# Gate of the DeltaNet group: tangent and products made per tile in the projection stage, squares and sums of its output norm per pair of tiles

## What is computed

```python
def deltanet_group(qkv, z, ab, ..., conv_w, a_log, dt_bias, norm_g, with_ctx_out):
    y = jax.nn.silu(short_conv(qkv_, conv_w))            # 5 taps over the tokens, 768 channels
    q, k, v = split(y);  q, k = l2norm(q) * 64 ** -0.5, l2norm(k)
    ...
    o_f, o_b = gated_delta_chunked(forward), gated_delta_chunked(flipped)
    def out(o, z_):                                      # o: 4 heads of 64
        o = rms_norm(o.transpose(0, 2, 1, 3), norm_g) * jax.nn.silu(z_).reshape(b_, t_, DN_HEADS, DN_HEAD_DIM)
        return o.reshape(b_, t_, DN_W)
    y = out(o_f + _flip_t(o_b), z)
```

## Time and profile before

| | us |
|---|---|
| median of 3 runs | 4419.28 (4417.69 to 4423.97) |
| the profiled execution | 4419.74 |
| span of its trace | 4417.9 |
| TensorE busy | 3963.3 (90%) |
| VectorE busy | 2058.3 (47%) |
| ScalarE busy | 1144.2 (26%) |
| GpSimd busy | 963.7 (22%) |
| mean granted TensorE clock | 0.942 of full |

### The profile page before, as it was taken

How to read it: one execution, slowest core, us unless ns; L and a number is a source line. 1 busy time by engine, 2 the same in 40 slices (tenths; PEclk the granted TensorE clock), 3 DMA queues, 4 the chain that set the end, 5 groups by cost and what they waited for, 6 DMA issues and landing times. The chain is left out here.

```text
span 4417.9 us, 77329 instructions
## 1 busy us (share of the span) xinstructions
PE 3963.3 (90%) x33040; PEld 3259.8 (74%) x33040; DVE 2058.3 (47%) x3681; ACT 1144.2 (26%) x2465; POOL 963.7 (22%) x671
## 2 busy tenths in 40 slices
PE   6999989789977999999996999889799788999997
PEld 4556877678865888888884657778688666888885
DVE  3344555444456433333356344566344554443346
ACT  3344223223322111111114443232233412111012
POOL 0000100033203333333321000100223114444441
PEclk8898999889988999999997999999799898999999
DMA  4211000100010111111111210000100010111111
GB/s 168 111 77 58 20 30 11 65 2 3 3 48 10 39 39 38 38 38 38 38 37 48 77 77 30 20 20 20 46 3 3 21 38 29 48 47 47 47 48 57
DMA packets 26495, 180.98 MB, mean 41 GB/s; under 512 B 2528, under 2 KB 4832, under 8 KB 10976
## 3 DMA queue, kind: packets, MB, share of 16 engines
q1 hardware_dynamic: 24912, 173.69, 10.6%
q10 hardware_dynamic: 1296, 3.10, 0.2%
HBM read 168.39 MB, written 8.39 MB: 40 GB/s over the span
## 5 line engine op out<-in xcount | busy, mean ns | idle before, releaser
L1291 PE MATMUL ps<-Yn_parts,ring_parts 128*128 128x512 f32 (+1 forms) x3840 | 802.1, 370 | 11.0 <-issue 7.7
L1291 PE MATMUL ps<-temp_parts,ring_parts 128*128 128x512 f32 (+1 forms) x2560 | 731.3, 371 | 55.8 <-DVE Hn_parts L2423 54.3
L1291 PEld LDWEIGHTS ps<-Yn_parts,ring_parts 128*128 128x128 f32 x3840 | 671.6, 190 | 138.3 <-issue 9.5
L1291 PEld LDWEIGHTS ps<-temp_parts,ring_parts 128*128 128x128 f32 x2560 | 468.1, 190 | 140.5 <-DVE Hn_parts L2423 55.7
L2694 POOL TENSOR_TENSOR ring_parts<-ring,consts 128x2048 fp32r<-128x2048 f32 x64 | 295.8, 4622 | 1200.9 <-DMA ring<-in_ff 1200.9
L735 PE MATMUL ps<-ring_parts,Xn_parts 128*128 128x256 f32 x2560 | 510.9, 295 | 51.4 <-DVE Hn_parts L1996 17.7
L2373 DVE SCALAR_TENSOR_TENSOR Xn<-ps,mods,Xn 128x256 f32<-128x256 f32 (+1 forms) x360 | 250.9, 697 | 623.1 <-PE ps L1291 514.3
L1291 PE MATMUL ps<-Hn_parts,ring_parts 128*128 128x512 f32 (+1 forms) x1280 | 473.7, 370 | 0.0
L735 PEld LDWEIGHTS ps<-ring_parts,Xn_parts 128*128 128x128 f32 x2560 | 423.3, 198 | 56.4 <-issue 37.0
L1818 ACT ACTIVATE Yn<-ps 128x256 f32<-128x256 f32 (+1 forms) x160 | 88.7, 554 | 1271.2 <-PE ps L1291 1271.2
L735 PE MATMUL ps<-ring_parts,Hn_parts 128*128 128x256 f32 x1280 | 370.4, 289 | 0.0
(11 more groups left out here) (312 smaller groups left out, 5982.8 us busy)
## 6 DMA issues: line engine op xcount, KB each, us to landing
ring<-in_ff SPq DMA_DIRECT2D x64, 1024.0 KB, 4.7
ring<-in_ada SPq DMA_DIRECT2D x22, 2048.0 KB, 8.5
ring<-in_halves SPq DMA_DIRECT2D x28, 1024.0 KB, 4.8
Xn<-in_x SPq DMA_DIRECT2D x2, 5120.0 KB, 25.1
Hn<-in_ada SPq DMA_DIRECT2D x2, 2048.0 KB, 20.9
kept_x<-Xn SPq DMA_DIRECT2D x4, 1024.0 KB, 4.0
Xn<-kept_x SPq DMA_DIRECT2D x1, 4096.0 KB, 15.4
out_x<-Xn SPq DMA_DIRECT2D x4, 1024.0 KB, 4.0
```

Source lines behind the costliest of these rows:

```text
L1291: m = pe.matmul(ps[:, bank, 0:hi - lo], w[a][:, k, j * P:(j + 1) * P], x[b][:, k, lo:hi], start=(k == 0 and part == 0), stop=(k == k_n - 1 ...
```

## The change

The copy of z on ScalarE becomes a tangent into a double buffer `z_th` (two tiles of 256 columns in a free part of `Yn`), which from tile 2 on waits for `z_sb` of tile t - 2. VectorE then does, in a new loop behind `silu(5)`, the product (tanh + 1) z from PSUM into `d_z`, linked, gives `z_sb`, and multiplies `d_z` by the gain. In the gate stage the tangent, both whole-tensor products and their waits are gone; squares and sums come in 5 pieces of 512 columns; `split_low` moves from ahead of the reciprocal to behind the third of the five pairs.

```diff
@@ dn_project, ScalarE
                     if t == 2:
                         squash(5)
                     act.wait_ge(sems["z_mm"], nth("z_mm", t + 1))
-                    A(d_z[:, t, :], ps[:, 4 + t % 2, 0:256], ACT.Copy).then_inc(sems["z_sb"], tally("z_sb"))
+                    if t >= 2:
+                        act.wait_ge(sems["z_sb"], nth("z_sb", t - 1))
+                    A(z_th[:, t % 2, :], ps[:, 4 + t % 2, 0:256], ACT.Tanh, scale=0.5).then_inc(sems["z_tanh"], tally("z_tanh"))
@@ gate, ScalarE
-                A(g_["sq"].rearrange("p a b -> p (a b)"), g_["o"], ACT.Square).then_inc(sems["sq_done"], tally("sq_done"))
-                A(flat(g_["th"]), flat(g_["z"]), ACT.Tanh, scale=0.5).then_inc(sems["g_tanh"], tally("g_tanh"))
+                for c in range(NT // 2):
+                    A(flat(g_["sq"][:, 8 * c:8 * c + 8, :]), g_["o"][:, 512 * c:512 * c + 512], ACT.Square).then_inc(sems["sq_done"], tally("sq_done"))
                 if g_ is gate_dn:
                     split_high()
@@ dn_project, VectorE
                 silu(5)
+                for t in range(NT):
+                    dve.wait_ge(sems["z_tanh"], nth("z_tanh", t + 1))
+                    link(STT(d_z[:, t, :], z_th[:, t % 2, :], 1.0, ps[:, 4 + t % 2, 0:256], ALU.add, ALU.mult))
+                    dve.sem_inc(sems["z_sb"], tally("z_sb"))
+                    z_ = d_z[:, t, :].rearrange("p (h c) -> p h c", h=H)
+                    TT(z_, z_, spread(par["dn_g"], 1, H), ALU.mult)
@@ gate, VectorE
-                heads, th = (lambda ap, n: ap.rearrange("p (h c) -> p h c", h=n)), flat(g_["th"])
-                n_gain = g_["gain"].shape[1]
-                dve.wait_ge(sems["sq_done"], nth("sq_done", 1))
-                link(dve.tensor_reduce(g_["root"], g_["sq"], AX.X, ALU.add))
+                heads = lambda ap, n: ap.rearrange("p (h c) -> p h c", h=n)
+                for c in range(NT // 2):
+                    dve.wait_ge(sems["sq_done"], nth("sq_done", c + 1))
+                    m = dve.tensor_reduce(g_["root"][:, 8 * c:8 * c + 8], g_["sq"][:, 8 * c:8 * c + 8, :], AX.X, ALU.add)
+                link(m)
                 TS(g_["root"], g_["root"], 1.0 / 64, EPS, ALU.mult, ALU.add).then_inc(sems["g_veps"], tally("g_veps"))
-                dve.wait_ge(sems["g_tanh"], nth("g_tanh", 1))
-                link(STT(th, th, 1.0, flat(g_["z"]), ALU.add, ALU.mult))
-                th_ = heads(th, NT * 256 // n_gain)
-                link(TT(th_, th_, spread(g_["gain"], 1, NT * 256 // n_gain), ALU.mult))
-                if g_ is gate_dn:
-                    split_low()
                 dve.wait_ge(sems["g_rstd"], nth("g_rstd", 1))
                 link(dve.reciprocal(g_["rs"], g_["root"]))
                 for c in range(NT // 2):
...
                     for a in range(2):
-                        m = STT(pairs(g_["out"], c)[:, a], o_[:, a], 0.5, pairs(g_["th"], c)[:, a], ALU.mult, ALU.mult)
+                        m = STT(pairs(g_["out"], c)[:, a], o_[:, a], 0.5, pairs(g_["z"], c)[:, a], ALU.mult, ALU.mult)
                     m.then_inc(sems["g_y"], tally("g_y"))
+                    if c == 2:
+                        split_low()
```

More of the change, by code:

```diff
@@ L226 @@
     "ln_sum", "ln_paired", "out_free", "ln_scaled", "fold", "h_seg", "x_seg",
-    "z_mm", "z_sb", "ss", "rstd", "normed", "cT_mm", "cT_sb", "up_mm", "up_v", "qk_roped", "qkT_mm", "qkT_sb",
+    "z_mm", "z_sb", "z_tanh", "ss", "rstd", "normed", "cT_mm", "cT_sb", "up_mm", "up_v", "qk_roped", "qkT_mm", "qkT_sb",
     "exped", "weighed", "y_done", "scores", "rowmax", "probs", "pT_mm", "pT_act", "pT_dve", "pv", "yT_mm", "yT_sb",
@@ L386, in build @@
         norm_segments = [(320 * s_, 320 * s_ + 320) for s_ in range(4)]
-        cv_y, _ = cut(Yn, 2 * NTOK, PADDED - 4)
+        cv_y, z_at = cut(Yn, 2 * NTOK, PADDED - 4)
+        z_th, z_at = cut(Yn, z_at, 2, 256)
+        assert z_at <= 4 * NTOK
         ringf = ring[:].rearrange("p a b -> p (a b)")
@@ L467, in gate_buffers @@
             out, at_ = {}, 0
-            for n_, shape in (("sq", (NT * H, 64)), ("th", (NT, 256)), ("out", (NT, 256)), ("root", (NT * H,)), ("rs", (NT * H,))):
+            for n_, shape in (("sq", (NT * H, 64)), ("out", (NT, 256)), ("root", (NT * H,)), ("rs", (NT * H,))):
                 out[n_], at_ = cut(region, at_, *shape)
```

## The result

The changed kernel takes **4435.82 us** (median of 9 runs, 4429.69 to 4438.68), the kernel before 4419.76 (9 runs, 4413.27 to 4424.86). The ratio is 1.0033, with a 95% interval of 1.0023 to 1.0043: slower by 10 to 19 us; the medians lie 16.1 us apart. The forecast was 4435.6. Its profiled execution took 4437.85 us for a span of 4436.1.

A forecast was written before the change was run, and what follows sets the result against it. TensorE, busy for 90% of the span, was taken as the bound. Per layer 7.7 + 2.2 + 1.0 - 2.8 = 8.1 us slower, 16.3 for two layers, gave 4435.6 us, range 4427 to 4441.

The forecast's parts named there:

- The wait for the bank: Projection: TensorE waits before z tile 2 for VectorE's first product behind silu(5); 7.7 us a layer lost.
- The clock: Projection: behind the 9.3 us gap TensorE runs at 1.2 GHz for a while; 2.2 us a layer lost, bounds 0 to 3.5.
- rival that the clock stays up: Projection: no clock drop behind the gap, so 2.2 us a layer are not lost; 4431.2 us, chance 0.13.
- The tail: Projection's end: tangent, product and gain behind the last tile replace a copy; 1.0 us more a layer, bounds 0.6 to 1.5.
- The pace of the small products: Projection: from tile 3 on TensorE sets the pace; tangent, product and gain take 1.42 us against 2.88 a tile.
- The gate stage: Gate stage: reciprocal about 5.0 us earlier, less 2.2 for split_low between pairs; net -2.8 us, bounds -5.0 to 0.
- Late next is that root: Gate stage: ScalarE's root, behind split_high's DMA wait and a table load, holds the reciprocal until 1242.90; VectorE idles about 4 us.
- worth nothing: Gate stage: squares and sums in five pieces end under the wait for the root, so they gain and cost nothing.
- the wait that doesn't bind: Projection rival: VectorE gives back the first banks in time, leaving the tail's 1.0 us a layer; 4415.8 us, chance 0.09.
- the gate that gives 5.0: Gate stage rival: the pause for split_low is hidden, so the gain is 5.0 us, not 2.8; 4431.2 us, chance 0.06.
- the gate that gives nothing: Gate stage rival: no gain there; 4441.2 us, chance 0.06 shared with the case of small products on the path.
- the small products on the path: Projection rival: VectorE's small products are not hidden under TensorE; 4441.2 us, chance 0.06 shared with the gate giving nothing.

The follow-up runs named there:

- e3: Changed kernel, but ScalarE copies z to SBUF, makes the tangent and frees the bank itself, and VectorE's products read the copies: 4418.93 us (ratio 0.9994).
- e8: Changed kernel with the products of z tiles 0 to 4 moved ahead of silu(5), between or behind the last convolution's taps, and squash(5) ahead of tile 5: 4411.69 us.
- e4: Changed kernel with 72 filler matmuls, whose results nobody reads, between z tile 1 and the wait before z tile 2: 4431.89 us (ratio 1.0025).
- e1: Projection stage of the changed kernel with the gate stage of the kernel before, so the gate is applied twice: 4441.52 us (ratio 1.0050).
- e5: Changed kernel with split_low back ahead of the reciprocal instead of between pairs 3 and 4: 4431.73 us (ratio 1.0028).
- e6: Changed kernel with ScalarE's square root ahead of both split_high, which wait for the weights' DMA: 4430.91 us (ratio 1.0022).
- e7: Changed kernel with one square and one sum over 2560 columns in place of five each: 4432.03 us (ratio 1.0025).
- e2: Gate stage of the changed kernel with the projection of the kernel before; tangent, product and gain left out altogether: 4412.81 us (ratio 0.9985).
- e11: The changed kernel as it is, timed again in a later group of runs: 4435.87 us (ratio 1.0035).

## Why the prediction was right

**The wait for the bank.** Forecast: tile 2 starts 12.14 us after the first z instruction (822.27 against 810.13), behind 9.3 us of idleness, 7.7 us lost. Measured: 12.04, 9.20 and 7.6. e3 and e8 show its cause from two sides. With another releaser the loss goes; with the same one ahead of `silu(5)` it goes as well.

**The clock.** Forecast 2.2 us a layer from the two rows at hand, 0 to 3.5 as bounds. Against e4 the changed kernel's trace lost 2.7 and 1.3, 2.0 in the mean. The forecast's 0.45 us lost per slow microsecond holds: 6.2 and 3.0 us at 1.2 GHz give 2.8 and 1.35. What it had too simple was the length of the slow stretch, one value for both layers. Six traces have the same gap of 9.2 us in both layers (the changed kernel twice, e1, e5, e6 and e7). Less e4's 37.8 us their twelve stages lost 1.3 to 2.7 us, 2.2 in the mean, so the one value was right as a mean. What sets the length of a single stretch is not shown by any run. The rival that the clock stays up is out: in none of the twelve was the gap free.

**The tail.** Forecast 1.0 us, measured 1.53 - 0.45 = 1.08.

**The pace of the small products.** Forecast hidden. From tile 4 on the tangents are 2.88 us apart, and VectorE idles 1.88 us for each. The Trainium skill (VectorE: DVE Perf Modes, The TRN2 errata) says that each instruction that reads SBUF pays a fixed extra latency, so that many small ones pay it many times. The trace agrees in the durations (ten of 0.42 us against one of 2.82), and the extra time has no weight here; e3 and e8 carry the same twenty instructions with a stage of 30.7 and 28.4 us.

**The gate stage.** Forecast -2.8 us; measured -3.0 and -2.9, and -2.93 twice in e2. The reciprocal came 5.2 and 5.1 us earlier where 5.05 and 4.96 were said, because the DMA landed 0.1 us sooner behind the first square. "Late next is that root" was shown by e6, the paid pause by e5, and "worth nothing" for the pairs by e7.

**The sum.** 8.1 us a layer was said, 7.6 stands in the two stages (15.3 for both layers), 16.1 us for both in the medians. The terms were right one by one; that the forecast of 4435.6 lies within 0.3 us of the median is luck, since the single runs of the changed kernel lie 9 us apart and its two medians, here and in e11, are 16.1 and 15.0 us above the kernel before.

Of the rivals, the wait that doesn't bind is refuted by the gap itself, the gate that gives 5.0 by e5, the gate that gives nothing by e2, the small products on the path by e3 and e8. One thing more stays open: why the untouched stages of one trace lie a few microseconds from those of another. Their clock switches at other places (from 600 to 780 us the mean granted clock is 0.95 in the trace before and 0.98 in the one after), but no run here fixes it.

## What to carry to other kernels

When a step moves from the engine that frees a buffer to one that is late, ask what stands ahead of it in that engine's queue at the moment the buffer is needed. Here 0.6 us of work stood behind 9 us of convolution and `silu(5)`, and the same work placed between two taps, with `squash(5)` moved behind tile 4 on ScalarE, cost TensorE no wait. And removing work from a busy engine gains only up to the next wait: before moving anything else, look for an instruction queued ahead of the releaser that waits for a DMA (here `split_high` before the root, 3.8 us).

## What the runs showed of the hardware

- The same idle time of 9.20 us cost 2.7 us in one layer and 1.3 in the other, by the time that the clock stayed at 0.50 behind it (6.2 and 3.0 us of work); over twelve such gaps it cost 1.3 to 2.7 us, 2.2 in the mean. With 72 filler matmuls in the gap the clock stayed at 1.00 and the cost was gone (e4).
- An idle time of 1.88 us amid dense matmuls was followed, once in two, by a drop of the clock to 0.50 that cost 1.5 us (e3).
- Stages with the same code repeat within 0.25 us over all traces as long as the clock does not move, while whole runs of one kernel differ by 3 to 22 us.
